# A softmax whose maximum is subtracted and whose inverse sum is applied on ScalarE, one head at a time

## The chip, the cores and the metric

The kernel runs on one core of a Trainium2 chip. A core has a matrix engine (TensorE, PE in the profile), a vector engine (VectorE, DVE), an engine for activation functions (ScalarE, ACT), a general engine that here mostly issues gathers (GpSimd, POOL), and queues that start DMA transfers. The metric is the device time of one execution in microseconds, lower is better. Shown times of the kernel before: median 2177.97 us of three runs (2165.36, 2177.97 and 2591.91).

## What is computed

One inference step of a decoder layer for 512 prompt tokens and 8 sequences of 8 new tokens, in float32. A token mixer runs an S5 state-space branch and a sliding-window attention beside each other, a layer norm follows, and then a PEER channel mixer: each token picks 128 rows of 1024 numbers out of `peer_u` and as many out of `peer_v`, by top-16 choices of keys. The change is in the attention's softmax, which has one more logit per head, the sink:

```
s = einsum(q, k) * HEAD_DIM ** -0.5, masked with -1e30
p = softmax(concatenate([s, sink], -1))[..., :-1]
o = einsum(p, v)
...
out = sum over 128 chosen rows:  gelu(peer_u[i] . x) * gate[i] * peer_v[i]
```

## The kernel before

The tokens stand in five tiles: tile 0 holds the 64 new tokens, tiles 1 to 4 hold 128 prompt tokens each. Tiles 1 and 0 are one group, tiles 2, 3 and 4 the other. A list written by `schedule()` (lines 58 to 111) orders the work, and each engine goes through that list in order and does its own part of every item; semaphores join them. An engine never goes past an instruction that waits.

First comes the token mixer of group one alone (state-space tables, scores, attention, gates, merge, output projection, layer norm), then the choice of rows for tile 1, and then the PEER stage. In that stage GpSimd issues one gather per row of `peer_u` (L500) and per row of `peer_v` (L507), VectorE makes one dot product per `peer_u` row (L1221), ScalarE turns four dots into their gelu (L1471), VectorE multiplies them by the gates (L1195), and ScalarE makes from each a diagonal matrix (L1465) with which TensorE adds up the `peer_v` rows (L795); some of these rows VectorE adds itself (L1211). Buffers for gathered rows are few, so that GpSimd waits for dots and for added rows. Between the steps of four rows of tiles 1 and 0 the list puts the whole token mixer of group two. The rows of tiles 2, 3 and 4 come after that.

Attention is computed in nine softmaxes: one for the new tokens (`ss`, 128 rows by 4 heads' parts by 192 columns), two for tile 1 in the first stage (`s`, j = 0), and six in the mixed stage (j = 1 to 3, two groups of heads each). Each of the eight for the prompt works on 128 by 4 by 256 scores. For one softmax VectorE takes the maximum over each head (L996), includes the sink (L997), forms sink minus maximum (L998), and subtracts the maximum from all scores (L999). ScalarE exponentiates the four sink terms (L1357) and then all scores in one instruction (L1358). VectorE sums (L1001, L1002), inverts (L1003) and multiplies all scores by the inverse sums (L1004). TensorE then transposes the probabilities (L671 and L675 for the new tokens, L706 for the prompt), ScalarE copies the transposed ones out of PSUM (L1271), and TensorE multiplies them with the values (L683, L684, or L713).

What ScalarE does after a softmax matters here. After those of the first stage its list has the sigmoids of four banks of gates (L1392, filled by TensorE at L726) and then the copies of the transposed probabilities. After those of the mixed stage it has the gelu of the last four dots (L1471), the diagonals (L1465), and then the copies. Exponential, sigmoid and gelu are in different tables, and an ACT_TABLE_LOAD stands ahead of the first use of each.

Of the kernel before, what the change touches and what calls it, by code (L numbers as in the profile page):

```python
# [9 lines left out]
ALU, ACT = mybir.AluOpType, mybir.ActivationFunctionType  # L10
# [202 lines left out]
def hybrid_step(nc, io):  # L213
# [5 lines left out]
    with ctx:  # L219
        def sb(name, shape, dt=F32):  # L220
            return ctx.enter_context(nc.sbuf_tensor(name, shape, dt))

        def sem(name):
            return ctx.enter_context(nc.semaphore(name))
# [10 lines left out]
        stat = sb("stat", [128, 80])  # L235
# [103 lines left out]
        roped = sem("rotary_done")  # L339
        scored = sem("scores_masked")  # L340
        expd_s = sem("exponentials_ready")
        probs = sem("probabilities_ready")
        sig = sem("gates_ready")
        merged = sem("merged_part_ready")
# [477 lines left out]
        def _(dve):  # L822
            V = nc.vector
            steps = [0]

            def step(ins):

                steps[0] += 1
                ins.then_inc(vstep, 1)
                dve.wait_ge(vstep, steps[0])  # L830
# [162 lines left out]
            def softmax(n, scores, sink, width, st):  # L993

                mx, ex, sm, rs = (stat[:, 8 * i:8 * i + width] for i in range(4))
                step(V.tensor_reduce(mx, scores, AX, ALU.max))  # L996
                step(V.tensor_tensor(mx, mx, sink, ALU.max))  # L997
                step(V.tensor_tensor(ex, sink, mx, ALU.subtract))  # L998
                V.tensor_tensor(scores, scores, mx.unsqueeze(2).broadcast_to([128, width, st]), ALU.subtract).then_inc(scored, 1)  # L999
                dve.wait_ge(expd_s, n)  # L1000
                step(V.tensor_reduce(sm, scores, AX, ALU.add))  # L1001
                step(V.tensor_tensor(sm, sm, ex, ALU.add))  # L1002
                step(V.reciprocal(rs, sm))  # L1003
                V.tensor_tensor(scores, scores, rs.unsqueeze(2).broadcast_to([128, width, st]), ALU.mult).then_inc(probs, 1)  # L1004
                dve.wait_ge(probs, n)

            masks, maskp = s("masks", 2, WIN + 64), s("maskp")

            def do_ss():
                for kv in range(2):  # L1010
                    for hf in range(2):
                        b = full(("ss", kv, hf))
                        drain(("ss", kv, hf), V.scalar_tensor_tensor(out=Psm[:, 2 * kv + hf, :], in0=b[:, 0:WIN + 64], scalar=HD ** -0.5,
                                                                     in1=masks[:, hf, :], op0=ALU.mult, op1=ALU.add))
                sk = stat[:, 60:64]
                step(V.tensor_copy(sk.rearrange("p (a b) -> p a b", a=2), s("sinks").unsqueeze(2).broadcast_to([128, 2, 2])))
                softmax(1, Psm, sk, 4, WIN + 64)
# [234 lines left out]
        def _(act):  # L1252
            S = nc.scalar
            steps = [0]

            def step(ins):
                steps[0] += 1
                ins.then_inc(astep, 1)
                act.wait_ge(astep, steps[0])
# [94 lines left out]

            def exponentials(n, scores, width):
                act.wait_ge(scored, n)
                step(S.activation(stat[:, 8:8 + width], stat[:, 8:8 + width], ACT.Exp))  # L1357
                S.activation(scores, scores, ACT.Exp).then_inc(expd_s, 1)  # L1358

            def do_ss():  # L1360
                exponentials(1, Psm, 4)
# [8 lines left out]
            def do_s(j, kv):  # L1370
                exponentials(1 + plan.index[("s", j, kv)], Pg[group(j + 1)], 4)
# [220 lines left out]
```

## Time and profile before

| | |
|---|---|
| median of three runs | 2177.97 us (2165.36 to 2591.91) |
| the profiled execution | 2157.18 us, its span 2155.4 us |
| DMA traffic | 675 MB, 313 GB/s over the span |
| chain that ended last | PE 29%, POOL 20%, issue 18%, DVE 15%, DMA 13%, ACT 2% |
| mean granted TensorE clock | 0.879 of full speed |

The first 400 us or so are the token mixer of the first group and the start of the gathers, 400 to about 550 us hold the six softmaxes of the second group, and from there on the gathers run nearly without a pause. Engine shares over the whole span mix these stages; the prediction goes by the stage.

### The profile page before, as it was taken

The page shows a single profiled execution, that of the slowest core. Times are in us where ns is not written, and L with a number is a line of the kernel's source. Part 1 is how long each engine was busy: PE and PEld are TensorE (multiplying, and loading weights), DVE is VectorE, ACT ScalarE, POOL GpSimd, SP SyncE. Part 2 cuts the span into 40 slices and gives each one's busy share as a digit, 9 for nine tenths or more (in the row PEclk, how much of TensorE's full clock was granted, in tenths as well). Part 3 has the DMA queues.
Part 4 walks back from the last instruction along what each step waited for, and adds up shares of the span by engine and source line. Part 5 has one row for each costly group of instructions (what it writes and reads, how often), then busy time and mean ns, then how long its engine had stood idle before and what let it go on. Part 6 is the DMA issues. An engine that isn't in the chain of part 4 may idle for free.

```text
span 2155.4 us, 16267 instructions
## 1 busy us (share of the span) xinstructions
PE 1581.4 (73%) x4705; PEld 797.3 (37%) x4705; DVE 1370.7 (64%) x3118; ACT 387.1 (18%) x905; POOL 1343.8 (62%) x1370
## 2 busy tenths in 40 slices
PE   6979986776987786876677675766675767776766
PEld 4667853444544332421232232322232322222222
DVE  7551237978989689858775666654476656444444
ACT  0222211223323122001111111111011121111111
POOL 0064004646667665777677777777777777667774
PEclk9979998878998898898889797989887889999998
DMA  5234346967999987999899999999989999999997
GB/s 213 90 78 119 124 141 219 347 216 267 356 367 379 373 310 272 400 351 370 292 371 373 356 371 358 364 383 367 391 328 357 358 356 389 367 362 373 380 369 269
DMA packets 186552, 675.05 MB, mean 313 GB/s; under 512 B 20960, under 2 KB 23440, under 8 KB 186048
## 3 DMA queue, kind: packets, MB, share of 16 engines
q0 software_dynamic: 167056, 609.25, 75.9%
q1 hardware_dynamic: 17632, 59.51, 7.7%
q10 hardware_dynamic: 1776, 5.24, 0.6%
q8 instruction: 39, 0.64, 0.1%
q14 instruction: 49, 0.40, 0.1%
HBM read 669.71 MB, written 3.69 MB: 312 GB/s over the span
## 4 chain that ended last, share of the span: by engine, by line
PE 29%; POOL 20%; issue 18%; DVE 15%; DMA 13%; another core or an unknown queue 2%; ACT 2%; ACTq 0%; SPq 0%; POOLq 0%; DVEq 0%
PE bank L795 15%; POOL region L507 7%; POOL region L500 6%; DMA region<-in_pv,region 6%; PE bank L726 4%; POOL wring L500 4%; DVE region L1221 2%; DMA discretisation<-in_pv,region 2%; DVE region L1211 2%; DMA wring<-in_pv,region 1%; DMA wring<-in_pu,region 1%; PE bank L547 1%; DMA region<-in_pu,region 1%; PE bank L747 1%
## 5 line engine op out<-in xcount | busy, mean ns | idle before, releaser
L795 PE MATMUL bank<-region,small 128*128 128x512 f32 (+1 forms) x1296 | 653.4, 650 | 281.3 <-ACT small L1465 123.0
L500 POOL DMA_INDIRECT region<-in_pu,region x348 | 390.6, 1122 | 292.2 <-DVE region L1221 103.4
L1221 DVE CUSTOM_DVE_ANT_0 region<-region 128x1024 f32<-128x1024 f32 x348 | 424.3, 1227 | 224.8 <-DMA region<-in_pu,region 199.3
L507 POOL DMA_INDIRECT region<-in_pv,region x392 | 442.5, 1129 | 163.3 <-issue 114.0
L795 PEld LDWEIGHTS bank<-region,small 128*128 128x128 f32 (+1 forms) x1296 | 248.8, 202 | 667.0 <-issue 546.0
L1221 DVE CUSTOM_DVE_ANT_0 wring<-wring,region 128x1024 f32<-128x1024 f32 x228 | 276.9, 1226 | 216.0 <-DMA wring<-in_pu,region 186.5
L500 POOL DMA_INDIRECT wring<-in_pu,region x228 | 238.4, 1046 | 69.5 <-issue 69.2
L1465 ACT ACTIVATE small<-small,region 128x128 f32<-128x128 f32 (+1 forms) x480 | 157.2, 387 | 667.5 <-DVE region L1195 241.3
L795 PE MATMUL bank<-discretisation,small 128*128 128x512 f32 (+1 forms) x196 | 117.9, 733 | 124.1 <-issue 65.4
L795 PE MATMUL bank<-wring,small 128*128 128x512 f32 x256 | 119.1, 599 | 22.7 <-DMA wring<-in_pv,region 15.4
L726 PE MATMUL bank<-xT,wring 128*128 128x192 f32 (+1 forms) x512 | 130.7, 417 | 0.0
L1471 ACT ACTIVATE region<-region 128x4 f32<-128x4 f32 x144 | 29.4, 204 | 519.2 <-issue 253.3
L726 PEld LDWEIGHTS bank<-xT,wring 128*128 128x128 f32 x512 | 94.2, 198 | 39.1 <-issue 7.3
L795 PEld LDWEIGHTS bank<-discretisation,small 128*128 128x128 f32 (+1 forms) x196 | 38.8, 213 | 188.5 <-issue 126.8
L1211 DVE SCALAR_TENSOR_TENSOR region<-region 128x1024 f32<-128x1024 f32 x66 | 84.9, 1287 | 18.4 <-issue 17.1
L795 PE MATMUL bank<-small 128*128 128x512 f32 (+1 forms) x172 | 87.6, 634 | 11.4 <-DMA small<-in_pv,region 7.2
L507 POOL DMA_INDIRECT small<-in_pv,region x60 | 68.8, 1146 | 26.1 <-issue 18.8
L507 POOL DMA_INDIRECT wring<-in_pv,region x64 | 69.9, 1093 | 19.5 <-issue 17.1
L507 POOL DMA_INDIRECT discretisation<-in_pv,region x60 | 65.3, 1089 | 25.0 <-issue 14.6
L795 PEld LDWEIGHTS bank<-wring,small 128*128 128x128 f32 x256 | 46.7, 190 | 91.7 <-issue 90.5
L747 PE MATMUL bank<-wring,region 128*128 128x512 f32 (+1 forms) x160 | 72.4, 612 | 9.3 <-DVE region L1069 9.3
L766 PE MATMUL bank<-xT,wring 128*128 128x192 f32 (+1 forms) x256 | 69.7, 433 | 1.4 <-ACT xT L1271 1.4
(244 smaller groups left out, 1709.8 us busy)
## 6 DMA issues: line engine op xcount, KB each, us to landing
wring<-in_w SPq DMA_DIRECT2D x104, 512.0 KB
region<-in_pv,region POOLq DMA_INDIRECT x392
region<-in_pu,region POOLq DMA_INDIRECT x348
wring<-in_pu,region POOLq DMA_INDIRECT x228
out_y<-region ACTq DMA_DIRECT2D x4, 512.0 KB
small<-in_small ACTq DMA_DIRECT2D x1, 1669.0 KB, 14.2
xT<-in_xT SPq DMA_DIRECT2D x1, 1536.0 KB, 20.0
region<-in_x SPq DMA_DIRECT2D x3, 512.0 KB, 16.7
```

Of the source, the lines that this page charges most:

```text
L500: pool.indirect_dma_start(ring_u[u_at.place[q]], None, io["pu"], bass.IndirectOffsetOnAxis(ind[:, k:k + 1], 0)).then_inc(g_u[u_at.place[q] ...
L507: pool.indirect_dma_start(ring_v[v_at.place[q]], None, io["pv"], bass.IndirectOffsetOnAxis(ind[:, k:k + 1], 0)).then_inc(g_v[v_at.place[q] ...
L547: last = mm(b[:, 0:cn], w[:, k, :], xT[:, k, c0:c0 + cn], start=k == 0, stop=k == KT - 1)
L726: last = mm(b[:, 0:cn], w[:, k0 + k, :], src[:, k, s0:s0 + cn], start=k == 0, stop=k == kn - 1)
L747: last = mm(b[0:tn, :], mTg[g][:, k, rel(t):rel(t) + tn], w[:, 512 * hf:512 * hf + 512], start=k == 0, stop=k == KT - 1)
L766: last = mm(b[:, 0:cn], w[:, k, :], xT[:, k, c0:c0 + cn], start=k == 0, stop=k == KT - 1)
L795: last = mm(bank[6 + hf][0:tn, :], diag[:, d % DIAGS, 0:tn], ring_v[v_at.place[q]][:, 512 * hf:512 * hf + 512], start=k == 0, stop=t not i ...
L1211: V.scalar_tensor_tensor(out=acc, in0=ring_v[v_at.place[q]], scalar=aact[:, n % 2, k:k + 1], in1=acc, op0=ALU.mult, op1=ALU.add).then_inc( ...
L1221: V.tensor_tensor_reduce(out=ring_u[u_at.place[q]], in0=ring_u[u_at.place[q]], in1=x1[t], scale=1.0, scalar=0.0, op0=ALU.mult, op1=ALU.add ...
L1465: S.activation(diag[:, d % DIAGS, 0:tn], eye, ACT.Copy, scale=aact[:, n % 2, k:k + 1]).then_inc(diag_s, 1)
L1471: S.activation(hact[:, n % 2, k], hdot[:, n % 2, k], ACT.Gelu).then_inc(act_s, 1)
```

## The change

The maximum is no longer subtracted from the scores by VectorE. VectorE negates the four maxima in place (a 128 by 4 instruction), and ScalarE passes them as the bias of the exponential; since the bias is one number per row, there is now one exponential per head, four in all. The inverse sums are no longer multiplied in by VectorE either: ScalarE does it, with four Copy activations whose scale is the inverse sum of the head. For this ScalarE waits, inside the softmax, for VectorE's sums. VectorE goes on after its reciprocal. The step that made the exponential of the scores wait for that of the sink terms is gone.

```diff
@@ softmax, VectorE
                 step(V.tensor_tensor(ex, sink, mx, ALU.subtract))
-                V.tensor_tensor(scores, scores, mx.unsqueeze(2).broadcast_to([128, width, st]), ALU.subtract).then_inc(scored, 1)
+                V.tensor_scalar(mx, mx, -1.0, None, ALU.mult).then_inc(scored, 1)
                 dve.wait_ge(expd_s, n)
                 step(V.tensor_reduce(sm, scores, AX, ALU.add))
                 step(V.tensor_tensor(sm, sm, ex, ALU.add))
-                step(V.reciprocal(rs, sm))
-                V.tensor_tensor(scores, scores, rs.unsqueeze(2).broadcast_to([128, width, st]), ALU.mult).then_inc(probs, 1)
-                dve.wait_ge(probs, n)
+                V.reciprocal(rs, sm).then_inc(inverse_s, 1)
+                dve.wait_ge(inverse_s, n)
@@ exponentials, ScalarE
                 act.wait_ge(scored, n)
-                step(S.activation(stat[:, 8:8 + width], stat[:, 8:8 + width], ACT.Exp))
-                S.activation(scores, scores, ACT.Exp).then_inc(expd_s, 1)
+                S.activation(stat[:, 8:8 + width], stat[:, 8:8 + width], ACT.Exp)
+                for i in range(width):
+                    last = S.activation(scores[:, i, :], scores[:, i, :], ACT.Exp, bias=stat[:, i:i + 1])
+                last.then_inc(expd_s, 1)
+                act.wait_ge(expd_s, n)
+                act.wait_ge(inverse_s, n)
+                for i in range(width):
+                    last = S.activation(scores[:, i, :], scores[:, i, :], ACT.Copy, scale=stat[:, 24 + i:25 + i])
+                last.then_inc(probs, 1)
```

On ScalarE, at the softmax of the new tokens in the first stage, before (region is the large work buffer, stat the small statistics, hgT and xT activations, bank a PSUM bank, small the constants):

```order
L1357 ACTIVATE stat<-stat 128x4 [waits scores_masked,bank_drained_by_scalar]
L1358 ACTIVATE region<-region 128x768 [waits scalar_step]
L1392 ACT_TABLE_LOAD [waits bank_drained_by_scalar,bank_filled,bank_drained_by_vector]
L1392 ACTIVATE region<-bank,small 128x192 [waits bank_filled]
L1392 ACTIVATE region<-bank,small 128x192 [waits bank_filled,bank_drained_by_scalar] x3
L1271 ACTIVATE region<-bank 128x512 [waits bank_filled,bank_drained_by_scalar]
```

and with the change (L1399 there is L1392 here):

```order
L1357 ACTIVATE stat<-stat 128x4 [waits scores_masked,bank_drained_by_scalar]
L1359 ACTIVATE region<-region,stat 128x192 x4
L1364 ACTIVATE region<-region,stat 128x192 [waits inverse_sums_ready,exponentials_ready]
L1364 ACTIVATE region<-region,stat 128x192 x3
L1399 ACT_TABLE_LOAD [waits bank_drained_by_scalar,bank_filled,bank_drained_by_vector]
L1399 ACTIVATE region<-bank,small 128x192 [waits bank_filled]
L1399 ACTIVATE region<-bank,small 128x192 [waits bank_filled,bank_drained_by_scalar] x3
L1271 ACTIVATE region<-bank 128x512 [waits bank_filled,bank_drained_by_scalar]
```

The load of the sigmoid's table and the four gates now stand behind the wait for VectorE's inverse sums and four more activations.

On ScalarE, at the third softmax of the mixed stage, before:

```order
L1357 ACT_TABLE_LOAD [waits scores_masked]
L1357 ACTIVATE stat<-stat 128x4 [waits bank_drained_by_scalar]
L1358 ACTIVATE region<-region 128x1024 [waits scalar_step]
L1471 ACT_TABLE_LOAD
L1471 ACTIVATE region<-region 128x4 [waits u_dot_done]
L1465 ACTIVATE small<-small,region 128x128 [waits v_rows_used,activation_ready]
```

and with the change (L1478 is L1471 here, L1472 is L1465):

```order
L1357 ACT_TABLE_LOAD [waits scores_masked]
L1357 ACTIVATE stat<-stat 128x4 [waits bank_drained_by_scalar]
L1359 ACTIVATE region<-region,stat 128x256 x4
L1364 ACTIVATE region<-region,stat 128x256 [waits inverse_sums_ready,exponentials_ready]
L1364 ACTIVATE region<-region,stat 128x256 x3
L1478 ACT_TABLE_LOAD
L1478 ACTIVATE region<-region 128x4 [waits u_dot_done]
L1472 ACTIVATE small<-small,region 128x128 [waits v_rows_used,activation_ready]
```

The gelu and the load of its table, which stood right behind the exponential, now stand behind the normalisation.

On VectorE, at the same kind of place in the mixed stage, with the change (ISA is the dot product of one gathered row and its accumulator read):

```order
L1000 TENSOR_SCALAR stat<-stat 128x4 [waits vector_step]
L1002 TENSOR_REDUCE stat<-region 128x4 [waits exponentials_ready]
L1003 TENSOR_TENSOR stat<-stat 128x4 [waits vector_step]
L1004 RECIPROCAL stat<-stat 128x4 [waits vector_step]
L1221 ISA region<-region 128x1024 [waits u_rows_in4,inverse_sums_ready]
L1221 ISA region 128x1
L1195 TENSOR_TENSOR region<-region 128x4 [waits gelu_ready]
```

Two full-width instructions have left VectorE. After the reciprocal it comes to one dot product, and then to the instruction that waits for ScalarE's gelu, in the same order as before.

## Rows read from the trace of the kernel before

**Rows 1.** The page: busy us (share of the span) x instructions, by engine.
```profile
PE 1581.4 (73%) x4705; PEld 797.3 (37%) x4705; DVE 1370.7 (64%) x3118; ACT 387.1 (18%) x905; POOL 1343.8 (62%) x1370
```

**Rows 2.** Windows: us, busy (x) per engine, then PEclk, DMA share, GB/s.
```profile
400.00:550.00 150.00, 106.52 (x342) 64.68 (x341) 123.94 (x239) 42.13 (x76) 84.55 (x72) 0.78 0.75 267
550.00:2155.40 1605.40, 1144.21 (x2584) 484.43 (x2582) 1045.07 (x2286) 272.28 (x687) 1152.70 (x1046) 0.88 0.95 358
```

**Rows 3.** Waits, 400 to 550 us: who waited for whom, us in total, times, longest.
```profile
POOL region L500 <- DVE region L1221: 39.1, 6, 9.9
```

**Rows 4.** Timeline of TensorE (first, third softmax): start us, us, engine, line, what, count, idle.
```profile
135.14 1.12 PE L671 MATMUL bank<-small,region 128*128 128x128 f32 x4 [12.17 <-DVE region L1004]
...
180.98 1.06 PE L713 MATMUL bank<-region 128*64 128x128 f32 x8 [1.05 <-ACT region L1271]
```

**Rows 5.** Timeline of ScalarE, four diagonals.
```profile
426.53 1.28 ACT L1465 ACTIVATE small<-small,region 128x128 f32<-128x128 f32 x4 [2.78 <-DVE region L1195]
```

**Rows 6.** Instructions of the softmax and the layer norm: ns min/median/max, first and last start.
```profile
L1080 DVE TENSOR_SCALAR stat<-stat x10: 145/154/155, 281.4 to 2148.3; 128x1 f32<-128x1 f32 x8, 64x1 f32<-64x1 f32 x2
L1004 DVE TENSOR_TENSOR region<-region,stat x9: 957/1224/1226, 134.1 to 528.7; 128x1024 f32<-128x1024 f32 x8, 128x768 f32<-128x768 f32 x1
L1358 ACT ACTIVATE region<-region x9: 843/1056/1057, 131.8 to 526.0; 128x1024 f32<-128x1024 f32 x8, 128x768 f32<-128x768 f32 x1
```

**Rows 7.** Timeline of ScalarE at the softmax of the new tokens.
```profile
132.70 1.28 ACT L1392 ACT_TABLE_LOAD   x1
134.00 1.78 ACT L1392 ACTIVATE region<-bank,small 128x192 f32<-128x192 f32 x4
136.35 0.60 ACT L1271 ACTIVATE region<-bank 128x512 f32<-128x512 f32 x1 [0.57 <-PE bank L671]
137.21 0.59 ACT L1271 ACTIVATE region<-bank 64x512 f32<-64x512 f32 x1 [0.26 <-PE bank L675]
```

**Rows 8.** Timeline of ScalarE at a softmax of the mixed stage.
```profile
463.64 0.21 ACT L1357 ACTIVATE stat<-stat 128x4 f32<-128x4 f32 x1
463.88 1.06 ACT L1358 ACTIVATE region<-region 128x1024 f32<-128x1024 f32 x1
464.95 1.28 ACT L1471 ACT_TABLE_LOAD   x1
466.25 0.20 ACT L1471 ACTIVATE region<-region 128x4 f32<-128x4 f32 x1
```

**Rows 9.** Timeline of VectorE at the same softmax.
```profile
461.05 1.22 DVE L999 TENSOR_TENSOR region<-region,stat 128x1024 f32<-128x1024 f32 x1
...
467.89 1.22 DVE L1221 CUSTOM_DVE_ANT_0 region<-region 128x1024 f32<-128x1024 f32 x1
...
469.05 0.16 DVE L1195 TENSOR_TENSOR region<-region 128x4 f32<-128x4 f32 x1
```

**Rows 10.** Timeline of ScalarE after the second softmax, and at the third.
```profile
164.49 0.42 ACT L1392 ACTIVATE region<-bank,small 128x192 f32<-128x192 f32 x1 [2.18 <-PE bank L726]
...
175.46 1.28 ACT L1392 ACT_TABLE_LOAD   x1
176.76 1.33 ACT L1392 ACTIVATE region<-bank,small 128x192 f32<-128x192 f32 x3
179.15 0.42 ACT L1392 ACTIVATE region<-bank,small 128x192 f32<-128x192 f32 x1 [1.06 <-PE bank L726]
179.61 1.23 ACT L1271 ACTIVATE region<-bank 128x512 f32<-128x512 f32 x2
```

**Rows 11.** Timeline: GpSimd ends the state recurrence (187.21); TensorE first uses it (192.47).
```profile
187.21 0.24 POOL L463 COPY fin<-region 128x32 f32<-128x32 f32 x1
...
192.47 0.38 PE L615 MATMUL bank<-region 128*72 128x128 f32 x2
```

**Rows 12.** Timeline of TensorE at a pause of the first stage.
```profile
230.17 5.18 PE L726 MATMUL bank<-hgT,wring 128*128 128x192 f32 x16 [3.18 <-issue]
...
236.49 2.76 PE L726 MATMUL bank<-hgT,wring 128*128 128x192 f32 x16
```

More of the change, by code:

```diff
@@ L341, in hybrid_step @@
         expd_s = sem("exponentials_ready")
+        inverse_s = sem("inverse_sums_ready")
         probs = sem("probabilities_ready")
```

## The prediction

> **What bounds the kernel now.** I read the page first for the shares of the engines [rows 1]. ScalarE is busy for 18% of the span and VectorE for 64%, so the change seems to move work from a full engine to an idle one. But that is a mean, and the nine softmaxes lie in two stages, so I read the windows next [rows 2]. From 550 us on the DMA engines are busy for 0.95 of the time: the gathers set the pace there, no softmax runs there, and a change of the earlier stages only shifts when that part begins. From 400 to 550 us they are busy for 0.75, and VectorE for 123.9 of 150 us. GpSimd stands still there for 39.1 us until VectorE has made a dot product [rows 3]; in the same list of waits VectorE waits for no transfer. So this stage goes by the chain VectorE, ScalarE, TensorE, VectorE. In the first stage the chain of waits runs mostly over TensorE, which waits at the attention for VectorE's softmax once and for ScalarE's copies [rows 4]. So what counts is, for each softmax, when the probabilities are ready, and when ScalarE comes to what stands behind it.
>
> **The cost of a per-head activation.** The trace has one of 128 columns with a scale out of memory, four in a row: 1.28 us [rows 5], that is 0.39 for the first and 0.30 for each more. A column costs (1056 - 843) / 256 = 0.83 ns [rows 6]. For 256 columns that makes 0.49 + 3 x 0.405 = 1.71 us for four heads, for 192 columns 0.44 + 3 x 0.35 = 1.49 us. That a bias out of memory costs what a scale does is an estimate. A bound from above is the gates, 128 by 192 with a bias: four in 1.78 us [rows 7], each waiting for the one before; with 64 more columns, 1.99. A bound from below is the single instruction over all columns, 1.06. I take 1.71, since neither the diagonals nor the new instructions wait for each other.
>
> **When the probabilities are ready (256 columns).** VectorE's subtraction (1.22) becomes a negation of four numbers, at most 0.155, the price of one number a row [rows 6]: -1.07. On ScalarE, from the start of the small exponential to the end of the large one, 0.24 + 1.06 = 1.30 us [rows 8] become about 0.11 + 1.71 = 1.82, since the step between them is gone: +0.52. The sum and the reciprocal stay. VectorE's multiplication (1.22) becomes four activations (1.71) and a hand-over of about 0.02: +0.51. Together -0.04: the probabilities come when they came. For the new tokens (192 columns a head) it is -0.80 + (1.60 - 1.08) + (1.51 - 0.96) = +0.27 us.
>
> **What stands behind them on ScalarE.** Before, ScalarE was free when its exponential ended; VectorE's sum, reciprocal and multiplication, 2.9 us, ran beside the load of the next table and the gelu. That cover is gone: ScalarE is now free when the probabilities are ready.
> - Mixed stage, six times. Before, the exponential ended at 464.94 [rows 8] and the probabilities were ready just ahead of the dot that started at 467.89 [rows 9], so ScalarE is free 2.9 us later, less 0.04. Table (1.28) and gelu (0.20) then end at about 469.33 instead of 466.45. VectorE is released 1.7 us earlier: 1.07 and 1.22 less, 0.52 more, and its first dot starts at about 466.2 instead of 467.89. It then needs the gelu, for the product that started at 469.05 [rows 9], and now gets it at about 469.38: +0.33 us. The diagonals wait for that product, the copies of the transposed probabilities for the diagonals, and TensorE, whose weighted sums and next scores VectorE waits for, for the copies: all +0.33. Of the 2.3 us taken off VectorE nothing is left, it becomes a wait for the gelu. Six times 0.33 is **+2.0 us**. The negation and the missing step are in it; the copies' own cost too.
> - New tokens. ScalarE is free at about 135.4 instead of 132.70. Table 1.28 and four gates 1.78 bring it to 138.5 [rows 7]; TensorE's transposes, which begin at 135.4 instead of 135.14 [rows 4], are done by then. The two copies (1.2 us) end at 139.7 instead of 137.8. TensorE waits for them: **+1.9 us**.
> - Second softmax. ScalarE comes back about 2.9 us later, with two banks of gates waiting, but the fourth is only filled at 164.49 [rows 10], over a microsecond after it has caught up. Nothing.
> - Third softmax. The load starts at 178.35 instead of 175.46; 1.28 and four gates of 1.78 end at 181.4, the two copies (1.23) at 182.65 instead of 180.84 [rows 10]. TensorE waited for these copies already [rows 4]: **+1.8 us**. GpSimd's recurrence for the state ends at 187.2 us and is needed at 192.5 [rows 11], so it hides nothing of this.
>
> Sum: 1.9 + 1.8 + 2.0 = **+5.7 us**, 0.26%. The gathers behind shift by the same.
>
> **A rule against the sum.** In the trace a table load lasts 1.28 us, begins 0.01 us after the exponential ends and the gelu follows it at once [rows 8]; so nothing but 1.28 is counted. The Trainium skill, "ScalarE: Activation LUTs", section "What ACT_TABLE_LOAD costs", adds a drain of about 1.38 us to each switch. By that rule, an estimate, the sum would be eight exposed switches of 1.38, some 11 us, higher; the trace does not agree with it. The same page of the Trainium skill, "Rules for kernel authors", sends multiplications to VectorE, for a speed in bf16; here, in float32, it is 1.71 us against 1.22.
>
> **Rivals.**
> - *The freed VectorE pays.* GpSimd restarts its gathers after the first dot of a step, now 1.7 us earlier, six times: 10.3 us. If late rows and not VectorE's order decide in the mixed stage, this comes off: 3.7 - 10.3 = -6.6 us. For it: 39.1 us of GpSimd's waits for dots [rows 3]. Against it: its transfers are at 0.75 and VectorE is never seen to wait for them; and the second dot comes 0.33 us later than before. Chance 0.15.
> - *Per-head activations overlap less.* They work in place, and a bias may be dearer. At 1.99 instead of 1.71 each softmax loses 0.56 more, eight of them on the path: +4.5, together +10. Chance 0.14.
> - *TensorE's clock falls in the longer pauses: slower than before.* After a pause of 3.18 us sixteen matmuls took 5.18 us instead of 2.76 [rows 12], the rate of the 1.2 GHz level against that of 2.4. At the third softmax the pause grows from 1.05 to 2.9 us, and the work behind it, at the 2.4 GHz level before, would start at the lower one. One such stretch costs 2.4 us: +8 together. In the mixed stage TensorE is busy for 106.5 us at 0.78 [rows 2]; were all of it at 0.5, it would be 166 us, and if all that lay on the path, +60 us. Only this could make it over 2% slower, from some 15 such stretches on; against it, the pauses there grow by 0.33 us only and the next work after most is at the low level already. Chance 0.12 for one or two stretches, 0.02 for more.
> - *A table switch costs more where it is newly exposed*: a load that was hidden could last longer than its row. For each of the eight, twice the row's 1.28 us would give +10, together +16. Every load in the trace lasts 1.283 us. Chance 0.01. The drain that the Trainium skill describes ("ScalarE: Activation LUTs", same section) would be such a mechanism.
>
> **The numbers.** The forecast, within a few microseconds of +5.7, has the rest, 0.56. The profiled execution took 2157.18 us, 20.8 below the median of three, which a far run of 2591.91 pulls up; the other two have a mean of 2171.8. With +5.7 I predict 2177 us; on the basis of the profiled execution it is 2163. The range takes in -6.6 and some 7 us by which runs differ downward (2158), and +16 with the upper one of the two near runs, 2178 (2194), and a few us of the clock (2200). A measurement of this kernel can tell about 2%, 43 us, from no change, and what leaves VectorE is some 20 us (8 x 2.3 and 1.8), so that even if all of it came off the path it would be 1%. Faster by over 2%: 0.02. Within 2%: 0.95. Slower: 0.03, the clock and what I don't see.
>
> **What would show it.** Right: the product L1195 starts some 2 us after the first dot ends, ended by ScalarE's gelu; the Copy activations last about 0.49 us, four of them 1.7; probabilities at the same distance from the maximum as before; TensorE's waits for L1271 at the first and third softmax are 1.8 us longer; VectorE's busy time 20 us lower, the span not. Wrong: if the gathers of the mixed stage end earlier and the span is shorter by over 5 us, VectorE's time was the pace after all; if four activations take over 2 us, their overlap was misjudged; if TensorE runs at half clock from 183 us on, the pause mattered.

## The result

| | median us | lowest to highest | runs | profiled execution, span |
|---|---|---|---|---|
| before | 2165.86 | 2145.23 to 2591.91 | 20 | 2155.4 |
| after | 2170.57 | 2160.89 to 2189.48 | 20 | 2160.5 |

Compared with each other, after takes **1.0047** of the time of before, 95% interval 1.0024 to 1.007: about 10 us more (5 to 15). That is far inside 2%, but the interval leaves out 1, so after is slower by a little. The two medians in the table are only 4.7 us apart, just under the lower end of that interval. The comparison leaves out the runs that are more than 1.5% above the fastest one of the same kernel, as the one of 2591.91 us. The predicted 2177 us lies in the range of the runs of both kernels. The sum had the right sign (+5.7 us) and about half the size.

The page of after, the line that answers to [rows 1]:

```profile
PE 1587.8 (73%) x4705; PEld 800.7 (37%) x4705; DVE 1350.7 (63%) x3109; ACT 406.3 (19%) x968; POOL 1320.6 (61%) x1370
```

VectorE is busy for 20.0 us less, ScalarE for 19.2 us more, and the span is 5.1 us longer. The windows of after (us, busy per engine, PEclk, DMA share, GB/s), against [rows 2]:

```profile
400.00:550.00 150.00, 107.96 (x324) 64.79 (x323) 101.22 (x204) 54.89 (x116) 74.17 (x69) 0.73 0.75 261
```

VectorE falls from 123.9 to 101.2 us of this window. Not all of that is the change: the softmaxes come some 4 to 9 us later, and with 35 instructions fewer in the window some of VectorE's other work has moved behind it. TensorE, with 18 matmuls fewer, is busy for 108.0 instead of 106.5 us, at a granted clock of 0.73 instead of 0.78. GpSimd's waits for dots in the same window, against [rows 3], and VectorE's new wait:

```profile
POOL region L501 <- DVE region L1221: 29.5, 10, 8.5
...
DVE region L1195 <- ACT region L1478: 10.4, 5, 2.1
```

GpSimd is released earlier, its waits are 9.6 us shorter in sum, and nothing ends sooner for it. VectorE has a wait that it did not have: 2.1 us, five times in this window, for the gelu (L1478 here). Timeline of VectorE in after at the softmax of [rows 9] (start, us, engine, line, what, idle and its releaser):

```profile
466.82 0.17 DVE L1000 TENSOR_SCALAR stat<-stat 128x4 f32<-128x4 f32 x1
...
471.86 1.23 DVE L1221 CUSTOM_DVE_ANT_0 region<-region 128x1024 f32<-128x1024 f32 x1
...
475.17 0.16 DVE L1195 TENSOR_TENSOR region<-region 128x4 f32<-128x4 f32 x1 [2.08 <-ACT region L1478]
```

ScalarE in after at the same softmax, against [rows 8]:

```profile
468.48 1.69 ACT L1359 ACTIVATE region<-region,stat 128x256 f32<-128x256 f32 x4
471.92 1.71 ACT L1364 ACTIVATE region<-region,stat 128x256 f32<-128x256 f32 x4 [1.75 <-DVE stat L1004]
473.64 1.28 ACT L1478 ACT_TABLE_LOAD   x1
474.93 0.20 ACT L1478 ACTIVATE region<-region 128x4 f32<-128x4 f32 x1
```

The order of the queue is what counts here. The table load and the gelu stand behind the four normalising activations, so the gelu starts at 474.93, and VectorE, whose dot started at 471.86, has been idle for 2.08 us when it gets it. The load lasts 1.28 us, as it did under cover, and the activations on either side stand next to it. The drain of about 1.38 us that the Trainium skill gives ("ScalarE: Activation LUTs", "What ACT_TABLE_LOAD costs") is not seen between these rows either.

The third softmax, ScalarE in after, against [rows 10]:

```profile
174.33 1.70 ACT L1364 ACTIVATE region<-region,stat 128x256 f32<-128x256 f32 x4 [1.79 <-DVE stat L1004]
176.05 1.28 ACT L1399 ACT_TABLE_LOAD   x1
177.35 1.78 ACT L1399 ACTIVATE region<-bank,small 128x192 f32<-128x192 f32 x4
179.16 1.23 ACT L1271 ACTIVATE region<-bank 128x512 f32<-128x512 f32 x2
```

and TensorE there, against [rows 4]:

```profile
176.51 1.04 PE L707 MATMUL bank<-small,region 128*128 128x128 f32 x8
180.53 1.94 PE L714 MATMUL bank<-region 128*64 128x128 f32 x8 [2.98 <-ACT region L1271]
182.40 12.65 PE L727 MATMUL bank<-xT,wring 128*128 128x192 f32 x64
```

The pause ahead of the weighted sums is 2.98 us instead of 1.05. Then comes what the sum had not counted: the same eight weighted sums take 1.94 us instead of 1.06, and the 64 matmuls behind them 12.65 us. In the trace of before these 64 are:

```profile
181.97 10.67 PE L726 MATMUL bank<-xT,wring 128*128 128x192 f32 x64
```

Windows of after behind that pause, columns as above:

```profile
181.00:184.00 3.00, 3.00 (x12) 2.67 (x12) 0.69 (x1) 0.00 (x0) 1.74 (x4) 0.50 0.37 72
184.00:187.00 3.00, 3.00 (x13) 3.00 (x12) 0.00 (x0) 0.00 (x0) 0.00 (x0) 0.59 0.79 239
187.00:190.00 3.00, 3.00 (x20) 3.00 (x19) 0.00 (x0) 0.47 (x2) 0.00 (x0) 1.00 0.54 150
```

TensorE is busy without a gap, at a granted clock of 0.50 (the 1.2 GHz level) and with 12 matmuls in 3 us, until past 186 us; then at 1.00 with 20.

**The stretches used below.** Whole times of one kernel spread by over 1% (2145 to 2178 us for before), more than the effect, so each trace is also measured by two stretches. *Stretch A*: from the start of the maximum of the first softmax (L996 in before) to TensorE's first use of the states (L615 in before). *Stretch B*: from the maximum of the fourth to that of the ninth softmax, five intervals. In us, worked out from the starts in the timelines (the last softmax of the mixed stage is the end of B, so five of the six forecast terms lie in it):

| kernel | A | of it: first to second max. | second to third | third to its weighted sums | from there to the states | B | its intervals |
|---|---|---|---|---|---|---|---|
| before | 63.4 | 23.11 | 17.76 | 11.08 | 11.49 | 103.4 | 23.97 17.39 20.27 23.89 17.89 |
| before_again | 63.0 | 23.10 | 17.28 | 11.08 | 11.50 | 103.7 | 23.98 15.48 20.27 23.89 20.03 |
| after | 69.2 | 25.10 | 16.73 | 13.01 | 14.36 | 108.8 | 24.22 19.34 20.62 24.22 20.41 |
| after_again | 69.4 | 25.10 | 16.74 | 13.03 | 14.57 | 107.1 | 24.23 17.64 20.63 24.22 20.40 |

By the means, A is 6.1 us longer and B 4.4: 10.5 us together, which lies in the 5 to 15 us of the ratio. The stretches ahead of A, and between A and the fourth softmax, differ by less than they do between two executions of one kernel. What follows the ninth softmax, the gathers, is no steady difference: after is 3.9 us shorter there in the first pair of traces (1630.1 against 1634.0) and 8.9 us longer in the second (1569.1 against 1560.2). So the two stretches show where time is lost, and that their sum is near the middle of the ratio's interval proves no more than that.

### The profile page after: what moved, and what is told of

It reads as the page before. It is cut to its first block, busy times and chain, and to the rows that moved or that the text cites. A ratio compares the mean times of both kernels' runs of the same rounds, so it can differ in the third digit from the quotient of the medians.

```text
span 2160.5 us, 16330 instructions
## 1 busy us (share of the span) xinstructions
PE 1587.8 (73%) x4705; PEld 800.7 (37%) x4705; DVE 1350.7 (63%) x3109; ACT 406.3 (19%) x968; POOL 1320.6 (61%) x1370
## 4 chain that ended last, share of the span: by engine, by line
PE 31%; POOL 25%; issue 17%; DVE 11%; DMA 11%; ACT 3%; another core or an unknown queue 2%; ACTq 0%; SPq 0%; DVEq 0%; POOLq 0%
PE bank L796 16%; POOL region L508 8%; POOL region L501 8%; DMA region<-in_pv,region 6%; POOL wring L501 5%; PE bank L727 3%; PE bank L640 2%; POOL wring L508 2%; POOL discretisation L508 1%; POOL small L508 1%; PE bank L548 1%; PE bank L748 1%; DVE region L1221 1%; DVE region L1211 1%
## 5 line engine op out<-in xcount | busy, mean ns | idle before, releaser
L501 POOL DMA_INDIRECT region<-in_pu,region x348 | 386.2, 1110 | 281.6 <-issue 99.6
L508 POOL DMA_INDIRECT region<-in_pv,region x392 | 432.4, 1103 | 187.5 <-issue 115.0
L1472 ACT ACTIVATE small<-small,region 128x128 f32<-128x128 f32 (+1 forms) x480 | 156.4, 387 | 648.5 <-DVE region L1195 271.0
L501 POOL DMA_INDIRECT wring<-in_pu,region x228 | 233.0, 1022 | 69.5 <-issue 69.2
L1478 ACT ACTIVATE region<-region 128x4 f32<-128x4 f32 x144 | 29.4, 204 | 516.9 <-issue 248.9
L796 PEld LDWEIGHTS bank<-wring,small 128*128 128x128 f32 x256 | 47.5, 194 | 106.5 <-issue 104.4
```

Source lines behind the costliest of these rows:

```text
L501: pool.indirect_dma_start(ring_u[u_at.place[q]], None, io["pu"], bass.IndirectOffsetOnAxis(ind[:, k:k + 1], 0)).then_inc(g_u[u_at.place[q] ...
L508: pool.indirect_dma_start(ring_v[v_at.place[q]], None, io["pv"], bass.IndirectOffsetOnAxis(ind[:, k:k + 1], 0)).then_inc(g_v[v_at.place[q] ...
L796: last = mm(bank[6 + hf][0:tn, :], diag[:, d % DIAGS, 0:tn], ring_v[v_at.place[q]][:, 512 * hf:512 * hf + 512], start=k == 0, stop=t not i ...
L1472: S.activation(diag[:, d % DIAGS, 0:tn], eye, ACT.Copy, scale=aact[:, n % 2, k:k + 1]).then_inc(diag_s, 1)
L1478: S.activation(hact[:, n % 2, k], hdot[:, n % 2, k], ACT.Gelu).then_inc(act_s, 1)
```

## The experiments

Twelve runs, in three groups of four; each group ran on one chip together with before, and ratios are to before in that group, with their 95% intervals. Whole times of different groups are not compared: before has a median of 2086.91, 2184.25 and 2182.92 us in them.

### Both kernels again, and each half of the change alone

*before_again* and *after_again* are the two kernels unchanged.

> The kernel before, once more, for a second trace of it. Theory A (order of work and clock): the first stage from the maximum of the first softmax to the first use of the states by TensorE (L615) takes 63.4 us again within 1 us, and the five intervals between the six softmaxes of the mixed stage sum to 103.4 us within 2 us; a ratio of 1.00. Theory B (the difference of 5 us between the two first traces is scatter of the executions): these two lengths differ from the first trace's by as much as those of the changed kernel did, 5.8 and 5.4 us.

> The changed kernel, once more, for a second trace of it. Theory A: the same two stretches take 69.2 us and 108.8 us again, within 2 us, with the work behind the third softmax (64 matmuls of L727) at about 12.6 us instead of 10.7; ratio 1.003 to 1.007. Theory B: the stretches fall between those of the two kernels, and the 64 matmuls take 10.7 us in one trace and 12.6 in another.

Measured: 0.9988 (0.9964 to 1.0012) and **1.0057** (1.0024 to 1.009). So the slowdown comes again on another occasion. The stretches come again to 0.1 us wherever TensorE's clock has no part (table above); intervals 2 and 5 of B don't, in either kernel.

*bias_only*: the maximum as a bias, VectorE normalises as before.

```
-  V.tensor_tensor(scores, scores, mx..., ALU.subtract)
+  V.tensor_scalar(mx, mx, -1.0, None, ALU.mult)
-  S.activation(scores, scores, ACT.Exp)
+  for i in range(width):
+      last = S.activation(scores[:, i, :], scores[:, i, :], ACT.Exp, bias=stat[:, i:i + 1])
```

> Only the first half of the change: the maximum is the bias of four exponentials, and VectorE multiplies by the inverse sums as before. Theory A (what costs is what stands behind the normalisation on ScalarE): the exponentials end 0.55 us earlier after the maximum, ScalarE is free at once, VectorE's product L1195 waits for nothing; 0.55 us less for each of six softmaxes, 0.3 for the new tokens: -3.6 us, ratio 0.998, never above 1.001. Theory C (four exponentials with a bias cost more than one, and that is the loss): +3 us or more, ratio 1.002 or above.

Measured: A 62.7, B 99.4 (intervals 23.42 17.18 17.83 23.40 17.58); ratio 1.0005 (0.998 to 1.003). In the undisturbed intervals 1 and 4 it is 0.55 and 0.49 us faster a softmax, what -1.07 + 0.52 gives. Of the 4 us that B is shorter, 2.4 are in the third interval alone; there the eight matmuls of L697 (L696 in before) take 1.99 us instead of 3.78, so that 1.8 of the 2.4 is TensorE's clock. Timeline of VectorE:

```profile
459.54 1.23 DVE L1005 TENSOR_TENSOR region<-region,stat 128x1024 f32<-128x1024 f32 x1
460.80 1.23 DVE L1222 CUSTOM_DVE_ANT_0 region<-region 128x1024 f32<-128x1024 f32 x1
...
461.95 0.16 DVE L1196 TENSOR_TENSOR region<-region 128x4 f32<-128x4 f32 x1
```

There is no wait ahead of L1196: the gelu was made while VectorE multiplied. This half of the change does no harm; whether its 4 us reach the end, the ratio can't tell.

*norm_only*: VectorE subtracts and one exponential does all heads, as before; ScalarE normalises head by head, as after.

```
-  V.tensor_scalar(mx, mx, -1.0, None, ALU.mult)
+  V.tensor_tensor(scores, scores, mx..., ALU.subtract)
-  for i in range(width): ... ACT.Exp, bias=...
+  S.activation(scores, scores, ACT.Exp)
```

> Only the second half: VectorE subtracts the maximum and ScalarE makes one exponential as before, and then the four Copy activations with the inverse sums as scale. Theory A: the probabilities come 0.5 us later, ScalarE is free 3.4 us later, the product L1195 comes 0.87 us later in each of the six softmaxes (5.2 us), the new tokens and the third softmax cost 2.2 and 2.4 us: +9.8 us, and with longer stretches at the lower clock +10 to +16; ratio 1.005 to 1.008. Theory C: without the exponentials per head, +2 to +4 us, ratio below 1.002.

Measured: A 67.4, B 108.8 (24.78 19.89 19.75 24.76 19.58); ratio **1.004** (1.0011 to 1.0068). VectorE at one of its mixed softmaxes:

```profile
468.18 1.23 DVE L1221 CUSTOM_DVE_ANT_0 region<-region 128x1024 f32<-128x1024 f32 x1
...
471.49 0.16 DVE L1195 TENSOR_TENSOR region<-region 128x4 f32<-128x4 f32 x1 [2.08 <-ACT region L1476]
```

The 2.08 us wait is the normalisation's alone, and intervals 1 and 4 are 0.8 us longer than in before. So the loss comes from the second half of the change; the first half pays back some of it. In one place it came out otherwise than in after: behind the third softmax the states are reached in 11.50 us. Its TensorE there:

```profile
183.05 1.06 PE L714 MATMUL bank<-region 128*64 128x128 f32 x8 [1.84 <-ACT region L1271]
184.04 10.67 PE L727 MATMUL bank<-xT,wring 128*128 128x192 f32 x64
```

The pause is 1.84 us, not 2.98, and the clock doesn't fall. But in the same trace it had fallen at the second softmax, with a pause that was shorter still (windows of TensorE alone: us, busy, PEclk, DMA share, GB/s):

```profile
165.97 1.06 PE L714 MATMUL bank<-region 128*64 128x128 f32 x8 [1.73 <-ACT region L1271]
168.33 12.01 PE L727 MATMUL bank<-xT,wring 128*128 128x192 f32 x64
```

```profile
165.00:170.00 5.00, 4.03 (x21) 0.77 0.24 85
```

There these 64 matmuls take 12.01 us, in after 10.67. So the length of a pause alone doesn't tell whether the clock falls.

### The order on ScalarE's queue

*gelu_first*: after, but in the mixed stage the normalisation stands behind the gelu. Nothing is added or removed.

```
+  def normalise(): (wait for the inverse sums, four Copy activations)
+  if n > 3: held.append(normalise)
+  else: normalise()
...
   (in do_peer, behind the gelu)
+  while held: held.pop()()
```

> The changed kernel, with one thing moved: in the six softmaxes of the mixed stage ScalarE loads the gelu's table and makes the gelu right behind the four exponentials, and the four Copy activations with the inverse sums only then. The first stage is that of the changed kernel. Theory A (the loss of the mixed stage is the gelu behind the normalisation): VectorE's product L1195 waits for nothing again, the six intervals lose 0.33 us each against the changed kernel and up to 1.2 more where TensorE was waited for: the five intervals sum to 98 to 103.5 us instead of 107 to 109, ratio to before 0.998 to 1.004, with the first stage still at 69 us. Theory C (the activations per head themselves are the loss): the intervals stay at 107 to 109, ratio 1.005.

Measured: A 69.3, B **99.2** (22.18 14.10 17.84 22.09 23.03); ratio 0.9983 (0.9946 to 1.0019). ScalarE and VectorE at a mixed softmax:

```profile
468.60 1.28 ACT L1487 ACT_TABLE_LOAD   x1
469.89 0.20 ACT L1487 ACTIVATE region<-region 128x4 f32<-128x4 f32 x1
470.34 1.71 ACT L1368 ACTIVATE region<-region,stat 128x256 f32<-128x256 f32 x4 [0.24 <-DVE stat L1004]
```

```profile
470.28 1.23 DVE L1221 CUSTOM_DVE_ANT_0 region<-region 128x1024 f32<-128x1024 f32 x1
471.43 0.16 DVE L1195 TENSOR_TENSOR region<-region 128x4 f32<-128x4 f32 x1
```

With the load and the gelu made beside VectorE's sum, the wait ahead of L1195 is gone, and intervals 1 and 4 are 1.8 us shorter than in before: 1.07 + 1.22 - 0.52 = 1.77. This is the gain that the change takes off VectorE, and with the other order all of it comes through in these two. So in the mixed stage the queue's order, not the price of the activations, turned it into a loss. (In interval 3 the eight L697 take 2.02 us instead of 3.78, as in bias_only: that part is the clock.) The first stage is untouched and still costs its 6 us, against the 4 that B gains. The last interval became 23.0 us: VectorE waits there for 7.00 us, until 524.28, for something that the profile can't name, 6.6 us after the weighted sums have ended. Why stays open.

*sum_on_act* and, again with the last group, *sum_again*: bias_only, and the exponentials also make the sums, so that VectorE's reduction goes.

```
-  step(V.tensor_reduce(sm, scores, AX, ALU.add))
   ... ACT.Exp, bias=stat[:, i:i + 1]
+  ... accum_out=stat[:, 16 + i:17 + i]
```

> The maximum as the bias of four exponentials, which also give the sum of their head (accumulator output); VectorE makes no sum over the scores and multiplies by the inverse sums itself. Theory A: the chain of each softmax on the path is shorter by 0.55 (bias) and 1.25 us (sum), less what an accumulator output costs, which no row shows: between nothing and 0.1 us a head. Five intervals of the mixed stage sum to 94 to 97 us instead of 103.5, the new tokens lose 1.2 us: -10 to -12 us, ratio 0.994 to 0.996. Theory E (time saved in these stages doesn't reach the end, since the gathers behind it take it up): the intervals shrink as said and the ratio is 0.998 to 1.001.

> The kernel with the sums out of the exponentials once more (bias and accumulator output on ScalarE, multiplication on VectorE), on another occasion: 0.994 of the kernel before again, within 0.003, if the gain of the two stages reaches the end; within 0.002 of 1 if not. First stage 61.5 us, the second, third and fourth interval of the mixed stage 14.1, 17.6 and 22.5 us.

Measured: A 61.6 and 62.9, B 99.0 and 100.8 (first interval 22.54 and 22.55); ratios **0.9939** (0.9904 to 0.9974) and **0.9956** (0.9933 to 0.9979). B is longer than the 94 to 97 us expected, and in sum_again the first stage and interval 2 (16.16 us) are longer than expected too. ScalarE in sum_on_act:

```profile
455.16 0.49 ACT L1359 ACTIVATE region<-region,stat 128x256 f32<-128x256 f32 x1
455.56 0.19 ACT L1359 ACTIVATION_READ_ACCUMULATOR region<-region,stat 128x1 f32 x1
455.65 0.49 ACT L1359 ACTIVATE region<-region,stat 128x256 f32<-128x256 f32 x1
```

From one head to the next it is 0.49 us instead of 0.40, since each sum has an instruction of its own: +0.36 us for four heads against a reduction of 1.22. Interval 1 is 0.87 us shorter than in bias_only (23.42 to 22.54), which is that difference.

### TensorE's clock at the third softmax

*warm_third*: after, with nine matmuls of 128 columns, whose result nobody reads, in the pause ahead of the third softmax's weighted sums.

```
+  if (j, kv) == (0, 1):
+      warm(b, 9)          # mm(b[:, 0:128], ident, ident, start=True, stop=True)
```

> The changed kernel with nine matmuls of the identity (2.3 us, result overwritten) in the one pause of 3.0 us between the transposes and the product with the values of the third softmax. Theory A (that pause lets TensorE's clock fall): the pause's end stays (13.0 us from the maximum to L714), the 64 matmuls behind take 10.7 us instead of 12.7 to 12.9, and the first stage 66.4 us instead of 69.3. Theory F (the clock falls there for another reason, such as the order of the work before): 12.7 us and 69.3 us again.

Measured: A **66.25** instead of 69.3, all of the difference behind the third softmax (from the weighted sums to the states 11.52 instead of 14.4); ratio 1.0014 (0.999 to 1.0038). TensorE:

```profile
178.92 2.17 PE L542 MATMUL bank<-small 128*128 128x128 f32 x18
181.97 1.09 PE L720 MATMUL bank<-region 128*64 128x128 f32 x8 [0.87 <-ACT region L1277]
182.98 10.67 PE L733 MATMUL bank<-xT,wring 128*128 128x192 f32 x64
```

ScalarE's copies end no earlier than in after (the third maximum to the weighted sums 12.92 against 13.01), but TensorE is idle for 0.87 us instead of 2.98, and the clock stays: 10.67 us, to the hundredth what before has.

*late_third*: before, with the first copy of the third softmax made four times instead of once on ScalarE; the change is not in it.

```
+  for _ in range(3 if (j, kv, i) == (0, 1, 0) else 0):
+      step(copy(PT[:, i]..., b[:, :]))
```

> The kernel before, with nothing of the change, but three added copies on ScalarE (1.9 us) ahead of the first copy of the transposed probabilities of the third softmax. TensorE's pause there becomes about 2.9 us instead of 1.05. Theory A: the first stage takes 1.9 us more for the copies and 2.9 for the clock, 68.2 instead of 63.0 to 63.4; the 64 matmuls take 12.7 us. Theory F: only the 1.9 us, 65.2 us in all, and 10.7 us for the matmuls.

Measured: A 66.8; ratio 0.9987 (0.9957 to 1.0017), in which 3.6 us can't be seen. TensorE, and a window of TensorE alone (us, busy, PEclk, DMA share, GB/s):

```profile
181.07 1.23 PE L713 MATMUL bank<-region 128*64 128x128 f32 x8 [2.94 <-ACT region L1271]
182.24 12.13 PE L726 MATMUL bank<-xT,wring 128*128 128x192 f32 x64
```

```profile
181.00:184.00 3.00, 2.93 (x14) 0.64 0.00 0
```

Lengthening this pause brings the fall: 1.9 us of wait, and 1.6 us for matmuls that run slower, without an instruction of the change. The expectation had 2.9 us for the clock and 68.2 us for A, so the size was missed. The eight weighted sums, right behind the pause, take 1.23 us here and 1.94 in after: the clock falls later. The two experiments show the cause from both sides.

### TensorE kept busy in the other pauses

*warm_before* and *warm_after*: 80 such matmuls ahead of the new tokens' probabilities, 12 ahead of those of each mixed softmax, and 6 ahead of the weighted sums of all eight softmaxes of the prompt.

> The kernel before, with matmuls of the identity by itself, whose result is overwritten, where TensorE waits at the attention: 80 before the probabilities of the new tokens, 12 before those of each softmax of the mixed stage, 6 before each product with the values. Theory A (pauses let TensorE's clock fall, and the work behind them pays): the products of the new tokens take under 10 us instead of 14, L713 and L696 of the mixed stage run at the rate of 2.4 GHz; first stage 63 to 56 us, intervals 103.5 to 90 to 100 us, ratio 0.988 to 0.995. Theory F (the low rate has another cause than the pause): no change of these rates, and what the added matmuls take is lost, ratio 1.00 to 1.01.

> The changed kernel with the same added matmuls. Theory A: without falls of the clock what is left between the two kernels is the waiting that the order of ScalarE's work makes: 1.9, 1.8 and six times 0.33 us, 5.7 in all, instead of the 10 to 12 that the traces show from the first softmax to the last. The 64 matmuls behind the third softmax take 10.7 us again. Theory F: the distance between warm_before and warm_after is 10 us or more, and these 64 matmuls take 12.6.

Measured: A 74.8 and 76.8, B 99.6 and 103.8; ratios 1.0002 (0.9968 to 1.0035) and 1.0027 (0.9993 to 1.0061). The 80 were too many:

```profile
125.81 20.53 PE L541 MATMUL bank<-small 128*128 128x128 f32 x160 [4.72 <-DVE region L1022]
```

Each is two records of 0.128 us on average, and they end at 146.3 us, 13 us after the probabilities are there (133.2): the new tokens' part can't be used, and A is over 10 us longer instead of 7 shorter. The rest can be used. The granted clock from 400 to 550 us is 0.92 in warm_before and 0.88 in warm_after, instead of 0.78 and 0.73. With the clock mostly held, after against before is +1.86 us from the third maximum to its weighted sums and nothing behind them (11.52 and 11.52), and of the five intervals of B four differ by **+0.18, +0.37, +0.36 and +0.32**, on average 0.31: the forecast term. The fourth differs by 2.9 us, and why isn't shown; TensorE waits in it for the diagonals, for 6.13 against 5.77 us, and has the added matmuls behind them.

*sum_warm*: sum_on_act with 34, 6 and 4 such matmuls, of the size of the pauses.

> The same kernel with added matmuls in TensorE's pauses, fewer than before: 34 before the probabilities of the new tokens (8.7 us), 6 before each softmax of the mixed stage (1.5 us), 4 before each product with the values (1 us). Theory A: none of them outlasts its pause; the narrow products of the new tokens begin at the high level and take 12 to 13 us instead of 14, L714 and L697 of the mixed stage run faster, together -5 to -10 us against the kernel without them; ratio to before 0.989 to 0.993. If the pauses are too short for them or the clock falls anyway: 0.994 to 0.998.

Measured: **0.9925** (0.9901 to 0.9949), 2166.47 us against 2182.92 on its chip; A 63.4, B 98.3. By the ratios it is the fastest kernel of this study, 16 us ahead of before. What the added matmuls give beyond sum_again's 0.9956 is not resolved, since the intervals overlap.

## Why the prediction was wrong, point by point

- **The bound** was read rightly: in the mixed stage the chain over VectorE and ScalarE sets the pace, and GpSimd's earlier restart is worth nothing (its waits for dots 9.6 us less, no span won). *The freed VectorE pays* is refuted for this order of the queue; in gelu_first 1.8 us come through in intervals 1 and 4, but no gain of the whole time that is clear of noise.
- **A per-head activation**: taken as 1.71 and 1.49 us for four, measured 1.69 to 1.71 and 1.47 to 1.49. *Per-head activations overlap less* is refuted. A bias costs what a scale does, here 1.69 and 1.71 us for four.
- **Mixed stage**: +0.33 forecast for each softmax; +0.25, +0.35 and +0.33 in intervals 1, 3 and 4, with the wait of 2.08 us ahead of L1195 as announced.
- **New tokens**: +1.9 forecast, +2.0 measured. **Third softmax**: +1.8 forecast, +1.94 measured (13.02 against 11.08), and the pause in front of L714 grew by 1.93.
- **Second softmax**: 0 forecast, -0.8 measured. In both traces of after the clock rose earlier in the matmuls of the gates there, 1.5 and 2.0 us after the second maximum began instead of 4.3 and 3.3; that was seen, not tested.
- **The step that failed** is the rival *TensorE's clock falls in the longer pauses*, which had 0.12 and was left out of the sum. At the third softmax it came exactly where it was placed, and it cost 2.97 us instead of the 2.4 given; the term in the sum was 0. No row gave a reason for putting it at nothing: the sum itself made the pause 2.9 us, and no row showed what follows a pause of that length. The row that the rival rested on was misread as well. [rows 12] give the price rightly, 5.18 us against 2.76, but not the cause: the clock hadn't fallen in the pause of 3.18 us (226.99 to 230.17). Windows of TensorE in before:

```profile
222.00:227.00 5.00, 4.25 (x39) 0.77 0.00 0
227.00:230.00 3.00, 0.00 (x0) 0.50 0.00 0
```

  A mean of 0.77 out of 1.00 and 0.50 puts the fall at about 224.7 us, while TensorE was busy with products of 72 columns (L627, from 223.74 on, after a pause of 0.74 us) and before the long pause began. The fall at the third softmax, though, came each time, in after, after_again and gelu_first. In the mixed stage the argument against it, that "the pauses there grow by 0.33 us only and the next work after most is at the low level already", held for three intervals and failed for two. TensorE, second interval, in before, before_again and after:

```profile
452.81 3.65 PE L713 MATMUL bank<-region 128*64 128x128 f32 x16 [2.25 <-ACT region L1271]
456.39 2.18 PE L696 MATMUL bank<-region 64*128 64x256 f32 x8
```

```profile
445.84 1.93 PE L713 MATMUL bank<-region 128*64 128x128 f32 x16 [2.47 <-ACT region L1271]
447.70 1.99 PE L696 MATMUL bank<-region 64*128 64x256 f32 x8
```

```profile
456.99 3.64 PE L714 MATMUL bank<-region 128*64 128x128 f32 x16 [1.96 <-ACT region L1271]
460.56 3.78 PE L697 MATMUL bank<-region 64*128 64x256 f32 x8
```

  These two groups stand on the edge already in before: they run at one level in one execution and at the other in the next. In after they run at the lower one more often; intervals 2 and 5 are 2 us and 0.4 to 2.5 us longer. The rows account for it: from the start of the first group to the end of the second it is 5.76 us in before and 7.35 in after, 1.59 of the 1.95 us by which interval 2 differs, and in interval 5 it is 5.27 and 7.35 us, 2.08 of 2.52. What is left, 0.36 and 0.44, is near the forecast term. In warm_after against warm_before the whole intervals differ by 0.37 and 0.32. That the change makes the low level more frequent here rests on two traces of each kernel. In late_third, which hasn't the change, interval 5 is 19.98 us, near the 20.03 of before_again, so two of three traces without the change are at the lower level there.
- **The account**: forecast terms 1.9 + 1.8 + five times 0.33 = 5.4 us; measured 10.5. The clock gives 3.0 in A, which two experiments show; 2.8 in B beyond the terms is put down to it by the rows above; the second softmax takes 0.8 away.
- **The number**: the base of 2171.8 us, a mean of two runs (2171.67 when worked out again), was 5.8 us above the median of twenty, and the sum was some 5 us short. The two errors cancel: 2165.86 and the 10 us of the ratio make 2176, next to the 2177 predicted. That is luck. The measured median, 2170.57, is 6 us lower, and the size of the effect was wrong.
- **A costlier table switch** is refuted: no load lasts longer than its 1.28 us.

**Open.** The last interval of B is 22 to 23 us in gelu_first and the two sum kernels, against 20.4 in after. The stretch between the first gather and the fourth softmax varies from 67 to 75 us between kernels that don't differ there, and what follows the ninth softmax varies by 9 us and more between executions, so a gain of 4 us in B is not found in the ratio of bias_only, and in gelu_first it stands against the 6 us of A. The sum kernels have ratios better than their stretches explain (6 us of A and B in sum_on_act, 13 by the ratio). An order with the normalisation behind the gates in the first stage wasn't tried.

## What to carry to other kernels

Work moved to an idle engine is paid by what stands behind it on that engine's queue: write down what that engine did while the other one worked (here a table load and a gelu, for nothing), and place the moved work behind it, as gelu_first does. When a forecast lengthens a pause of TensorE, read the granted clock in short windows around the pauses that the trace has, see whether it fell in the pause or while TensorE was busy, and put the slower matmuls into the sum and not among the rivals. If the exponential goes head by head anyway, let it make the sum as well: only the kernels that did so had a ratio below 1 that was clear of noise.

## What the runs showed of the hardware

- **TensorE's clock and a pause.** At the third softmax, with pauses of 2.98, 3.00 and 2.94 us (after, after_again, late_third) the granted clock fell to the 1.2 GHz level in the pause or just behind it; with 1.05 and 1.84 us (before, norm_only) it stayed at 2.4. With a pause of 0.87 us behind 2.17 us of matmuls that nobody reads (warm_third) it stayed, too. At the second softmax of norm_only it fell after 1.73 us. The work before the pauses was not the same everywhere, so this is no threshold.
- **The clock also fell while TensorE was busy.** Timeline of warm_before at the new tokens, 3 us behind a pause of 1.02 us (147.2 to 148.24):

```profile
151.21 0.31 PE L689 MATMUL bank<-region,hgT 64*64 64x32 f32 x2
151.45 0.42 PE L688 MATMUL bank<-region 128*64 128x32 f32 x2
151.80 0.42 PE L689 MATMUL bank<-region,hgT 64*64 64x32 f32 x2
```

  From 148.24 us on TensorE makes nothing but products of 32 columns, without a pause. At first they take 0.30 us a pair, and from 151.45 us on 0.42. The granted clock is 1.00 from 140 to 150 us and 0.50 from 152 to 160. In before it fell the same way at 224.7 us, in products of 72 columns.
- **The sum beside an activation.** It is an instruction of its own (0.187 us) and costs 0.09 us of ScalarE's time a head: 0.36 us for four, against 1.22 for their reduction on VectorE.
